# Projections spread over a pair's steps in a hybrid attention and PEER block, with two smaller edits

## The reference, cut to what matters

```python
z = x @ w_in                          # queries, keys, values of both head groups
y_fox = fox_attention(fq, fk, fv, log_f)        # 8 heads, causal, with a decay bias
y_swa = swa_sink_attention(sq, sk, sv, sink)    # 8 heads, window of 128, a sink each
x = layer_norm(ALPHA * x + concat(y_fox, y_swa) @ w_out)
q = x @ w_pq                          # 8 retrieval heads, two halves of 128
# the best 16 of 128 keys per half, then the best 16 of 256 sums -> experts e, gates g
a = gelu(sum_d u_tab[e] * x) * g
x = layer_norm(ALPHA * x + sum_e a * v_tab[e])
```

## Time and profile before

| | us |
|---|---|
| three runs | 1682.19, 1684.14 (median), 1688.33 |
| the profiled execution | 1689.24 |
| its span | 1687.6 |
| TensorE matmuls busy | 1570.4 (93%) |
| VectorE busy | 1306.9 (77%) |
| GpSimd busy | 1092.4 (65%) |
| ScalarE busy | 664.6 (39%) |
| mean granted TensorE clock | 0.969 |

### The profile page before, as it was taken

The page is one execution under the profiler, slowest core; times in us unless marked ns, Lnnn a source line. Parts: engine busy times, 40 slices in busy tenths (PEclk is TensorE's granted clock), DMA queues, the critical chain, the costliest instruction groups (busy, mean ns, idle before and its releaser), DMA issues.

```text
span 1687.6 us, 25879 instructions
## 1 busy us (share of the span) xinstructions
PE 1570.4 (93%) x8005; PEld 1346.3 (80%) x8005; DVE 1306.9 (77%) x2075; ACT 664.6 (39%) x1018; POOL 1092.4 (65%) x847
## 2 busy tenths in 40 slices
PE   7978878889999999899999999789999999999994
PEld 4656656678898999899999999767777777777773
DVE  4344343620398999999999997389999999999998
ACT  4544444333333333245555555223333333333332
POOL 3221122633458888776665557788888888888885
PEclk9989889989999999999999999999999999999997
DMA  5110211322258888787888888979999999999991
GB/s 214 44 50 26 75 50 50 125 100 87 91 169 279 265 295 284 244 283 268 296 286 295 302 312 322 343 263 344 336 346 333 341 335 345 331 341 334 346 326 51
DMA packets 156301, 402.06 MB, mean 238 GB/s; under 512 B 13088, under 2 KB 77344, under 8 KB 154080
## 3 DMA queue, kind: packets, MB, share of 16 engines
q1 hardware_dynamic: 118800, 267.13, 45.0%
q0 software_dynamic: 37456, 134.37, 23.1%
HBM read 351.31 MB, written 50.14 MB: 238 GB/s over the span
## 4 chain that ended last, share of the span: by engine, by line
PE 81%; POOL 7%; DVE 5%; issue 3%; ACT 3%; DMA 1%; ACTq 0%; POOLq 0%; SPq 0%; DVEq 0%
PE banks L1328 13%; PE banks L1330 12%; PE banks L1329 12%; PE banks L1382 12%; PE banks L1383 11%; PE banks L1384 11%; POOL lo L331 4%; PE banks L1582 3%; PE banks L1581 2%; PE banks L1445 2%; POOL rows L544 2%; ACT hi L326 1%; PE banks L1428 1%; DVE probs L937 1%; PE banks L1522 1%
## 5 line engine op out<-in xcount | busy, mean ns | idle before, releaser
L331 POOL TENSOR_TENSOR lo<-raw,hi 128x1024 fp32r<-128x1024 f32 x306 | 737.9, 2412 | 496.7 <-ACT hi L326 494.4
L326 ACT ACTIVATE hi<-raw 128x1024 fp32r<-128x1024 f32 x306 | 323.1, 1056 | 386.0 <-PE banks L1384 384.8
L1328 PE MATMUL banks<-x1T_hi,hi 128*128 128x384 f32 (+2 forms) x1168 | 409.9, 351 | 32.7 <-POOL lo L331 29.7
L1329 PE MATMUL banks<-x1T_lo,hi 128*128 128x384 f32 (+2 forms) x1168 | 400.6, 343 | 0.0
L1330 PE MATMUL banks<-x1T_hi,lo 128*128 128x384 f32 (+2 forms) x1168 | 400.4, 343 | 0.0
L1239 DVE TENSOR_TENSOR wgt_lo<-wgt,wgt_hi 128x384 fp32r<-128x384 f32 x128 | 309.1, 2415 | 18.8 <-ACT wgt_hi L822 12.9
L1382 PE MATMUL banks<-hi,wgt_hi 128*128 128x512 f32 x768 | 310.9, 405 | 0.7 <-POOL lo L331 0.7
L1383 PE MATMUL banks<-lo,wgt_hi 128*128 128x512 f32 x768 | 304.3, 396 | 0.0
L1384 PE MATMUL banks<-hi,wgt_lo 128*128 128x512 f32 x768 | 303.9, 396 | 0.0
L1328 PEld LDWEIGHTS banks<-x1T_hi,hi 128*128 128x128 f32 x1168 | 222.8, 191 | 50.3 <-POOL lo L331 21.6
L1330 PEld LDWEIGHTS banks<-x1T_hi,lo 128*128 128x128 f32 x1168 | 223.0, 191 | 4.9
(11 more groups left out here) (179 smaller groups left out, 2003.9 us busy)
## 6 DMA issues: line engine op xcount, KB each, us to landing
raw<-u_t SPq DMA_DIRECT2D x128, 512.0 KB, 5.0
raw<-v_tab SPq DMA_DIRECT2D x128, 512.0 KB, 6.1
g_scratch<-stage SPq DMA_DIRECT2D x12, 2048.0 KB, 7.4
gg<-g_scratch SPq DMA_DIRECT2D x32, 768.0 KB, 10.9
gelu_scratch<-gelu SPq DMA_DIRECT2D x116, 192.0 KB, 4.1
ga<-gelu_scratch SPq DMA_DIRECT2D x29, 768.0 KB, 7.4
raw<-w SPq DMA_DIRECT2D x34, 512.0 KB, 3.3
raw<-w_pq SPq DMA_DIRECT2D x16, 512.0 KB, 3.2
```

Of the source, the lines that this page charges most:

```text
L326: act.activation(hi[c % PART_SLOTS][:, :], raw[:, c % RAW_SLOTS, :], ACT.Copy).then_inc(hi_ready, 1)
L331: eng.tensor_tensor(lo[c % PART_SLOTS][:, :], raw[:, c % RAW_SLOTS, :], hi[c % PART_SLOTS][:, :].bitcast(F32), ALU.subtract).then_inc(lo_r ...
L1328: pe.matmul(o, h[:, s], hiT[:, k, tokens], start=(k == 0), stop=False)
L1329: pe.matmul(o, h[:, s], loT[:, k, tokens], start=False, stop=False)
```

## The change

It consists of four groups of edits.

- **Attention.** `PROJ_AT` now begins the projections at steps 1, 4, 10 and 13, three steps each. `COPY_AT` puts ACT's copies at steps 8, 9, 13 and 16, and DVE's low parts one step later. `ROUND_AT` puts ACT's roundings at steps 1, 4, 7 and 13. Projections 0 and 1 stay in their banks until steps 8 and 9.
- **Gathers.** The expert numbers are copied eight columns at a time into one of two buffers; POOL's loops run over two octets.
- **Late expert tiles.** The low parts of tiles 117, 119, 121, 123 and 125 are made by DVE after the dots of ranks 104, 108, 113, 118 and 119. SP loads the first two gate groups after the load of tile 123 instead of after that of tile 127.
- **Norms.** One-number steps are `tensor_scalar` with pointer operands. The second norm works in the banks; block 2's gain and bias move from POOL to DVE, all of DVE's finishing for blocks 2 and 3 comes after the statistics of block 3, and blocks 2 and 3 are stored in halves.

```diff
@@ -74,6 +74,9 @@
+SPLIT_BY_DVE = {117: 104, 119: 108, 121: 113, 123: 118, 125: 119}
@@ -153,7 +156,7 @@
-        expert_at = [sb(f"expert_at{i}", [P, 1], U32) for i in range(ROWS)]
+        expert_at = [sb(f"expert_at{i}", [P, ROWS], U32) for i in range(2)]
@@ -331,6 +334,10 @@
+        def in_turn(eng, c):
+            eng.wait_ge(lo_ready, c)
         def units():
@@ -353,12 +360,16 @@
-        PROJ_AT = {8: (0, 3), 11: (1, 3), 14: (2, 3), 17: (3, 2)}
+        PROJ_AT = {1: (0, 3), 4: (1, 3), 10: (2, 3), 13: (3, 3)}
+        COPY_AT = {8: 0, 9: 1, 13: 2, 16: 3}
+        ROUND_AT = {1: 5, 4: 6, 7: 7, 13: 8}
...
-        SHARED_X, SHARED_Y = (2,), (0, 1, 2)
+        SHARED_X, SHARED_Y = (2,), (0, 1)
...
         def shared_norm(n):
@@ -426,13 +437,6 @@
-            for it in range((A_PRE + A_MID) // 4, ETILES // 4 - 1):
-                for k in range(4):
-                    load_tile(sp, S_U + 4 + k, it, u_t[4 * it + (4 + k)])
-            for half in range(2):
-                sp.wait_ge(gelu_stored[half], 16 * (A_PRE + A_MID) // 2)
-                sp.wait_ge(g_stored[half], 16 * CHUNKS // 2)
             def load_group(g, slot):
@@ -443,8 +447,17 @@
-            load_group(KEPT_FROM, 0)
-            load_group(KEPT_FROM + 1, 1)
+            for it in range((A_PRE + A_MID) // 4, ETILES // 4 - 1):
+                for k in range(4):
+                    load_tile(sp, S_U + 4 + k, it, u_t[4 * it + (4 + k)])
+                if it == (A_PRE + A_MID) // 4:
+                    for half in range(2):
+                        sp.wait_ge(gelu_stored[half], 16 * (A_PRE + A_MID) // 2)
+                        sp.wait_ge(g_stored[half], 16 * CHUNKS // 2)
+                    load_group(KEPT_FROM, 0)
+                    load_group(KEPT_FROM + 1, 1)
@@ -460,15 +473,21 @@
-            for b in (0, 1, 3, 2):
-                if b in SHARED_Y:
-                    sp.wait_ge(shared_done, shared_norm(TB + b) + 1)
-                else:
-                    sp.wait_ge(y_ready, 1)
+            def store_halves(b, before):
+                for h in range(2):
+                    sp.wait_ge(y_ready, before + h + 1)
+                    sp.dma_start(out[bass.ts(b, P), bass.ts(h, 512)], x1[:, b, bass.ts(h, 512)]).then_inc(out_stored, 16)
+            def store_block(b):
+                sp.wait_ge(shared_done, shared_norm(TB + b) + 1)
...
-            sp.wait_ge(out_stored, 16 * TB)
+            store_block(0)
+            store_halves(2, 0)
+            store_block(1)
+            store_halves(3, 2)
+            sp.wait_ge(out_stored, 16 * 6)
@@ -524,46 +543,67 @@
-            def gather(table, ks, r, tile=None, split_first=False):
-                if split_first:
+            def gather(table, ranks, r, tile, split_first=False):
+                even = r if isinstance(r, int) else 0
+                if split_first and tile is not None:
+                    if tile[0] - S_U - 1 in SPLIT_BY_DVE:
+                        in_turn(pool, tile[0])
...
-                first = 0 if table is u_rows else RANKS
-                for k in ks:
+                for k in ranks:
...
-                    pool.tensor_copy(expert_at[k % ROWS][:, :],
-                                     expert[:, bass.ds(ROWS * r + (k - first), 1)]).then_inc(expert_at_ready, 1)
-                pool.wait_ge(expert_at_ready, ROWS * r + (ks[-1] + 1))
+                    if k % ROWS == 0:
+                        column = ROWS * r + (k if table is u_rows else k - RANKS)
+                        pool.tensor_copy(expert_at[(even + k // ROWS) % 2][:, :],
+                                         expert[:, bass.ds(column, ROWS)]).then_inc(expert_at_ready, 1)
+                        pool.wait_ge(expert_at_ready, r + (k // ROWS + 1))
...
-                for k in ks:
-                    at = bass.IndirectOffsetOnAxis(ap=expert_at[k % ROWS][:, :], axis=0)
+                for k in ranks:
+                    numbers = expert_at[(even + k // ROWS) % 2]
+                    at = bass.IndirectOffsetOnAxis(ap=numbers[:, k % ROWS:k % ROWS + 1], axis=0)
...
-                ks = [2 * k, 2 * k + 1] if k < AHEAD else [k + AHEAD]
-                gather(u_rows, ks, 0, (S_U + 8 * O_IDLE + k, 0))
-            with pool.Fori(1, R_PRE + R_MID) as r:
+                ranks = [2 * k, 2 * k + 1] if k < AHEAD else [k + AHEAD]
+                gather(u_rows, ranks, 0, (S_U + 8 * O_IDLE + k, 0))
+            def u_octet(first, r):
...
-                    gather(u_rows, [k + AHEAD], r, (S_U + 8 * O_IDLE + k, 2 * r))
+                    gather(u_rows, [first * ROWS + k + AHEAD], r, (S_U + 8 * (O_IDLE + first) + k, 2 * r))
+            assert (R_PRE + R_MID) % 2 == 0
+            u_octet(1, 0)
+            with pool.Fori(1, (R_PRE + R_MID) // 2) as i:
+                u_octet(0, 2 * i)
+                u_octet(1, 2 * i)
...
-                gather(u_rows if rank < RANKS else v_rows, range(rank, rank + n), 0, (S_U + k, 0), split_first=True)
+                gather(u_rows if rank < RANKS else v_rows, range(rank, rank + n), 0,
+                       None if k in SPLIT_BY_DVE else (S_U + k, 0), split_first=True)
...
-            with pool.Fori(0, OCTETS - 1) as o:
+            def v_octet(first, o):
...
-                    gather(v_rows, [k + AHEAD + RANKS], o, (S_V + k, 2 * o))
+                    gather(v_rows, [RANKS + first * ROWS + k + AHEAD], o, (S_V + 8 * first + k, 2 * o))
+            assert OCTETS % 2 == 0
+            in_turn(pool, S_V)
+            with pool.Fori(0, OCTETS // 2 - 1) as i:
+                v_octet(0, 2 * i)
+                v_octet(1, 2 * i)
+            v_octet(OCTETS - 2, 0)
@@ -631,8 +671,6 @@
-                if k < 3:
-                    split_hi(act, S_LOOP + k + 2, j)
@@ -643,9 +681,11 @@
+            split_hi(act, S_LOOP + 3, 0)
...
+            split_hi(act, S_LOOP + 4, 0)
@@ -681,17 +721,16 @@
-                    if step == 1:
-                        split_hi(act, S_LOOP + 5, j)
+                    if step in ROUND_AT and not (last and step > 1):
+                        split_hi(act, S_LOOP + ROUND_AT[step], j)
...
-                    for begin, (k, n) in PROJ_AT.items():
-                        if not last and step == begin + n:
-                            projected(k, j + 1)
+                    if step in COPY_AT and not last:
+                        projected(COPY_AT[step], j + 1)
@@ -717,7 +756,8 @@
-                act.activation(x1[:, b, :], y0 if n == TB else x1[:, b, :], ACT.Identity, bias=rstd[:, b, 5:6],
+                source = x1[:, b, :] if n < TB else banks[:, 2 * b:2 * b + 2, :].rearrange("p h n -> p (h n)")
+                act.activation(x1[:, b, :], source, ACT.Identity, bias=rstd[:, b, 5:6],
@@ -946,11 +986,8 @@
-                    for begin, (k, n) in PROJ_AT.items():
-                        if not last and step == begin + n:
-                            projected_lo(k, j + 1)
-                if not last:
-                    projected_lo(3, j + 1)
+                    if step - 1 in COPY_AT and not last:
+                        projected_lo(COPY_AT[step - 1], j + 1)
@@ -977,7 +1014,7 @@
             def begin_norm(b, n):
...
-                    ins = dve.bn_stats(stats[:, b, h, :], banks[:, h, :] if n == TB else x1[:, b, bass.ts(h, 512)])
+                    ins = dve.bn_stats(stats[:, b, h, :], banks[:, 2 * b + h, :] if n >= TB else x1[:, b, bass.ts(h, 512)])
@@ -990,17 +1027,35 @@
-                chained(dve.scalar_tensor_tensor(t, r0, v, r0, ALU.mult, ALU.mult))
+                chained(dve.tensor_scalar(t, r0, v, r0, ALU.mult, ALU.mult))
...
-                chained(dve.tensor_tensor(r1, r0, t, ALU.mult))
+                chained(dve.tensor_scalar(r1, r0, t, None, ALU.mult))
...
-                    dve.scalar_tensor_tensor(rstd[:, b, 5:6], moments[:, b, 0:1], -1.0, r1,
-                                             ALU.mult, ALU.mult).then_inc(factors_ready, 1)
+                    dve.tensor_scalar(rstd[:, b, 5:6], moments[:, b, 0:1], -1.0, r1,
+                                      ALU.mult, ALU.mult).then_inc(factors_ready, 1)
...
-                chained(dve.scalar_tensor_tensor(x1[:, b, :], x1[:, b, :], moments[:, b, 0:1], gb[:, 0, :],
+                if n < TB:
+                    chained(dve.scalar_tensor_tensor(x1[:, b, :], x1[:, b, :], moments[:, b, 0:1], gb[:, 0, :],
+                                                     ALU.subtract, ALU.mult))
+                    dve.scalar_tensor_tensor(x1[:, b, :], x1[:, b, :], r1, gb[:, 1, :],
+                                             ALU.mult, ALU.add).then_inc(done, 1)
+                    return
+                chained(dve.scalar_tensor_tensor(sums(b), sums(b), moments[:, b, 0:1], gb[:, 0, :],
...
-                dve.scalar_tensor_tensor(x1[:, b, :], x1[:, b, :], r1, gb[:, 1, :],
-                                         ALU.mult, ALU.add).then_inc(done, 1)
+                for h in range(2):
+                    half = bass.ts(h, 512)
```

(22 more changed lines are left out.)

## The result

The changed kernel took 1640.75 us (median of 4 runs, 1639.23 to 1641.61) beside 1685.45 for the one before (4 runs, 1682.19 to 1688.33): a ratio of 0.9734, 95% interval 0.9713 to 0.9755, or 44.7 us less. The forecast was 57 less. The profiled execution took 1641.61, its span is 1639.9 and its mean granted clock 0.983 (0.969 before).

The account below looks back on a forecast made before the run. PE was taken to bound the kernel, by its waits and low-clock time. Savings of 28 + 4 + 3.5 + 16 + 5.5 = 57 us took the median from 1684.14 to 1627 us, range 1610 to 1654.

Parts of the forecast that it names:

- Late expert tiles: Tile 119 to the first value tile: DVE's splits and earlier gate loads save 16 us, bounds 5 and 18.9.
- rival (b): Late expert tiles: DVE's splits wait for gathers behind gate loads, gain 5 instead of 16, 1638 us; chance 0.15.
- Gathers: Expert gathers up to 1040 us: fewer index copies and loop turns save 3.5 us, bounds -2 and 11.4.
- Attention: Attention pairs: moved projections and copies save 9.0 us in each of three, 1 in the last; 28 us, bounds 0 and 50.
- The middle wait: Attention steps 7 to 9, without projection: PE waits 3.9 us a pair behind ACT's eight copies, before the third projection.
- Rival (a): Bare copies: attention steps 7 to 10 cost 9 us a pair, not 3.9; attention gives 10, 1645 us; chance 0.20.
- Rival (c): Full clock: attention pairs run at 2.4 GHz and reach 48.5 us, 15 more gained, 1612 us; chance 0.11.
- First norm: Norm between the stages: one-number DVE steps no longer held by POOL, 4 us saved, bounds 0 and 5.6.
- End: Second norm and last stores: faster one-number steps and a halved last store save 5.5 us, bounds -2 and 7.
- (d): Attention pairs: the low clock holds throughout, slower than before, 68 us more, 1752 us; chance 0.03.
- (e): Whole kernel: PE waits simply move with the work, time within 8 us of 1684; chance 0.03.

Follow-up runs that it names:

- norms alone: The kernel before with only the pointer steps, the second norm in the banks and the halved stores: 1675.01 us, ratio 0.9942.
- the run with a split before the decay loads: Changed kernel with gate loads behind the last u tile and POOL splitting tile 6 before waiting for the eighth logits: 1626.16 us, ratio 0.9653 to the kernel before.

## Why the prediction was right, and where it was not

The forecast of 1627 was 13.8 us too low, inside its range of 1610 to 1654. The sign and the main term held; the sum of 57 was made of one term far too large and one too small. That the attention's surplus of 7.7 made up for part of what the late tiles lacked is luck.

- **The step that failed: "Late expert tiles", "16 us".** Its stretch measured 4.4, and the changed kernel without the two late edits has the same 69.5 us there and the same ratio, so they gave nothing that can be told. In price it is near rival (b), the late tiles wait for data, with its 5, but not in place: (b) put waits of 2 to 3 us at five DVE tiles behind gathers, and one of them has such a wait; the largest stands before a u tile behind the gate loads. The step had the danger in its last sentence (1.5 MB of gate loads beside gathers and u tiles) and left 2.9 us of waiting for it; the waits are 13.2 (1.32 + 2.87 + 5.69 + 3.29). It also counted both edits in full, though neither gains beside the other: without DVE's splits the changed kernel is as fast, and with them the early loads cost 3 us over late ones.
- **"Gathers", 3.5:** 0 in the stretch that it spoke of, where PE's waits for POOL stayed at 11.0 us in nine pieces. The copies that went had likely stood in tiles where PE did not wait for POOL; no run has this edit alone. In the late tiles, to which the term gave nothing, each short wait shrank by some 0.4; by the medians the edit is worth 1.5, within the noise.
- **"Attention", 28:** 35.7 in the profile, 33.3 alone. By its own parts, for the second and third pair: content 44.7 forecast and 45.8 measured (47.4 busy less 0.03 x 52), waits 3.9 + 1.5 = 5.4 and 4.6, clock 3.5 and 1.6. The middle wait was there, but of another cause and at another place: PE waits for probabilities behind DVE, not for ACT's copies before the third projection. I had ACT's eight copies as the bound and the two blocked DVE steps fitting under them; it is the other way round, and the run with a split before the decay loads shows it. The last pair gained 6.0 and not 1: I kept the split over the second scaling, which is now just ahead of it (2.2), and left out the clock, from 0.83 to 1.00 over some 28 us (4.8 at most). Rival (a), bare copies, did not come: no pair shows 9 us there. Rival (c), full clock with pairs of 48.5, is not this kernel but is the one with the moved split, at 48.6 and 48.7 for two of its pairs.
- **"First norm", 4, and "End", 5.5:** 2.7 (with some of the gathers in it; 1.3 for norms alone) and 6.3, together 9.7 alone against 9.5. The end came out by two errors: the chain up to DVE's last operation gave 4.3 for 5.3, and what follows it 1.9 for 0.3. A step with a pointer operand was taken at 0.15 and takes 0.21 to 0.27, so it is not held. The page "VectorE: DVE Perf Modes" of the Trainium skill, section "Mode 2×_2P — use both read ports for one tensor", lets an SBUF `tensor_scalar` use both read ports, and the prediction took from it that these steps could be locked out. The trace shows that they are not; the section splits the outermost dimension that is not one, and a single number per partition has none, so it does not speak of them. What the first norm's term left out is that DVE, faster through the small steps, meets POOL in the large ones.
- **The low clock through the pairs (d) and "it does not do what it says" (e):** neither; the clock of the pairs is 0.94 to 0.97. The point from which (d) decides is a little off: 50.1 + 21 is 8.5 above the pair of now and not 8.7, and to outweigh the other terms' 29 it takes 9.7 a pair, so 22 us at the low clock. The chances of the forecast, (a), (b) and (c) add up to 0.94, not 0.93.
- **Of the signs named:** pairs of 52 to 56, a clock over 0.9, one wait of 2 to 4, none over 1 at a pair's start, DVE's gate wait gone, 14 to 16 us at the end: all there, 51.8 a hair under. ACT's eight copies back to back are not there, and the wait is not before the third projection. One-number steps at 0.15 hold for the norms only nearly (up to 0.27), and in the pairs steps of up to 3.13 are left. The first value tile 15 to 18 us closer to tile 119 is not there either (1.8), and DVE's tiles show the wait of 3 that was named as the sign of failure.

## What to carry to other kernels

Edits that bear on the same stretch don't add up: here DVE's splits alone brought 2 to 4 us, the early loads alone none that can be told, and both together none either, so try each without the other, and neither, before keeping both. A wait that is gone is not yet time gained. An early load is paid by whatever load stands behind it in its queue: move it ahead only by as much as the queue has room for; here two groups cost 3 to 4 us and one cost nothing that can be told. And where two engines lock each other out, look at which of them holds several operations back behind an unrelated wait (here two splits behind four decay loads): putting one ahead of the wait was worth a fifth of the whole change.

## What the runs showed of the hardware that was not expected

A one-number DVE step with one tensor input, immediate or pointer operand, is not held by a POOL operation (0.15 us with immediates, 0.21 or 0.27 with pointers; one of 0.21 inside POOL's 2.34), while one with two tensor inputs lasts until POOL's operation ends, through two of them in a row (3.13 us for one number). Large operations of both engines with two inputs each wait for the other's to end: 3.24 us for DVE's and 3.20 for POOL's where 1.28 and 2.34 stand alone. When the scaling begins just ahead of a POOL split it can go either way: with a lead of 0.04 to 0.06 us it took 0.35 us thirteen times and 2.53 to 2.59 five times in the traces of this case, with 0.17 or 0.18 it took 0.35 all twelve times. The two gate loads keep SP for 10.71, 10.32 and 6.54 us at their early place, in three traces, while the u tiles' loads and the gathers are under way, and for 1.96 to 7.24 at their late one, in ten. The first of them lands 14.2 to 19.9 us after its issue at the early place and 7.5 to 18.6 at the late one.
